# The V stage and the final norm of a hybrid block, token by token

## What is computed

```
q = (hf @ w_q).reshape(t, 8, 2, 128); s = einsum(q, sub_keys)
# per head: top 16 of each half, top 16 of their 256 sums -> 128 experts a token, of 16384
act = gelu(einsum('td,tkd->tk', x, u[idx]))
out = einsum('tk,tkd->td', gate * act, v[idx])
return rmsnorm(x + out, final_norm_w)
```

## Time and profile before

| | us |
|---|---|
| median of 3 runs | 5157.62 |
| the profiled execution | 5157.0 |
| its span, first to last instruction | 5155.2 |
| TensorE matmul busy in it | 4926.2 |
| VectorE busy | 3193.6 |
| ScalarE busy | 1684.1 |
| GpSimd busy | 1115.2 |

### The profile page before, as it was taken

The page is one execution under the profiler, slowest core; times in us unless marked ns, Lnnn a source line. Parts: engine busy times, 40 slices in busy tenths (PEclk is TensorE's granted clock), DMA queues, the critical chain, the costliest instruction groups (busy, mean ns, idle before and its releaser), DMA issues. The chain is left out here.

```text
span 5155.2 us, 69591 instructions
## 1 busy us (share of the span) xinstructions
PE 4926.2 (96%) x25836; PEld 4445.1 (86%) x25836; DVE 3193.6 (62%) x4382; ACT 1684.1 (33%) x1716; POOL 1115.2 (22%) x454
## 2 busy tenths in 40 slices
PE   6999988999999899998969999999999899999997
PEld 5878767888888787787759999999999799999997
DVE  3566666888888100101038866666776688888886
ACT  2222323333333222222223248885222222222222
POOL 2433320000000344343334430001221111111111
PEclk6999989999999999999989999999999999999998
DMA  1222212222222332334223357778997888888884
GB/s 71 90 90 77 90 57 82 78 87 77 77 87 71 124 109 104 144 122 157 98 99 110 116 206 284 276 274 315 337 341 293 298 299 296 298 299 300 302 301 151
DMA packets 230894, 913.34 MB, mean 177 GB/s; under 512 B 18352, under 2 KB 100912, under 8 KB 152624
## 3 DMA queue, kind: packets, MB, share of 16 engines
q1 hardware_dynamic: 193968, 644.12, 35.0%
q0 software_dynamic: 36864, 268.45, 14.6%
HBM read 837.00 MB, written 75.50 MB: 177 GB/s over the span
## 5 line engine op out<-in xcount | busy, mean ns | idle before, releaser
L158 POOL TENSOR_TENSOR ring_low<-ring_raw,ring_high 128x2048 fp32r<-128x2048 f32 x167 | 777.2, 4654 | 2178.9 <-ACT ring_high L153 2178.9
L176 PE MATMUL rt_acc<-h_high,ring_high 128*128 128x384 f32 (+1 forms) x2304 | 789.9, 343 | 0.7 <-POOL ring_low L158 0.7
L177 PE MATMUL rt_acc<-h_low,ring_high 128*128 128x384 f32 (+1 forms) x2304 | 784.4, 340 | 0.0
L178 PE MATMUL rt_acc<-h_high,ring_low 128*128 128x384 f32 (+1 forms) x2304 | 784.2, 340 | 0.0
L153 ACT ACTIVATE ring_high<-ring_raw 128x2048 fp32r<-128x2048 f32 x337 | 645.6, 1916 | 391.2 <-PE out_acc L178 125.1
L176 PEld LDWEIGHTS rt_acc<-h_high,ring_high 128*128 128x128 f32 x2304 | 433.1, 188 | 10.9 <-POOL ring_low L158 1.0
L177 PEld LDWEIGHTS rt_acc<-h_low,ring_high 128*128 128x128 f32 x2304 | 433.1, 188 | 9.9
L178 PEld LDWEIGHTS rt_acc<-h_high,ring_low 128*128 128x128 f32 x2304 | 432.8, 188 | 10.1
L176 PE MATMUL hg_acc<-h_high,ring_high 128*128 128x512 f32 x1024 | 408.1, 399 | 9.2 <-DVEq L968 9.2
L178 PE MATMUL hg_acc<-h_high,ring_low 128*128 128x512 f32 x1024 | 401.0, 392 | 0.0
L177 PE MATMUL hg_acc<-h_low,ring_high 128*128 128x512 f32 x1024 | 399.7, 390 | 0.0
(11 more groups left out here) (300 smaller groups left out, 10136.8 us busy)
## 6 DMA issues: line engine op xcount, KB each, us to landing
ring_raw<-u_tiles SPq DMA_DIRECT2D x128, 1024.0 KB, 5.1
ring_raw<-v_tiles SPq DMA_DIRECT2D x128, 1024.0 KB, 5.8
ring_raw<-w_hg SPq DMA_DIRECT2D x64, 1024.0 KB, 4.8
ring_raw<-w_ssd SPq DMA_DIRECT2D x48, 1024.0 KB, 4.8
ring_raw<-w_mix_s SPq DMA_DIRECT2D x32, 1024.0 KB, 4.8
ring_raw<-w_mix_h SPq DMA_DIRECT2D x32, 1024.0 KB, 4.8
gelu<-sb_rt_gelu SPq DMA_DIRECT2D x128, 192.0 KB, 5.1
gates<-sb_rt_table SPq DMA_DIRECT2D x12, 2048.0 KB, 7.7
```

The costliest lines, as they stand in the source:

```text
L158: nc.gpsimd.tensor_tensor(ring.low[:, slot], ring.raw[:, slot], ring.high[:, slot].bitcast(F32), ALU.subtract).then_inc(ring.low_ready, 1)
L176: nc.tensor.matmul(out, high[:, m], x_high[:, k, tokens], start=(k == 0), stop=False, skip_group_check=True)
L177: nc.tensor.matmul(out, high[:, m], x_low[:, k, tokens], start=False, stop=False, skip_group_check=True)
L178: last = nc.tensor.matmul(out, low[:, m], x_high[:, k, tokens], start=False, stop=(k == KT - 1), skip_group_check=True)
```

## The change

The V stage and the final norm work with tokens on partitions: `x_tok` is `[128, 4 token blocks, 2048]`. In the V stage w's 128x128 blocks (keys by tokens) are the stationary side and 512 columns of v the moving one, so a half has 6 outputs (3 token blocks by 2 pieces of 512 features) in place of 8, over eight banks in turn. The gathered rows are added right into `x_tok`'s block 0. The out stage turns each x_mid tile by four transposes and stores it to DRAM as `x_tok`, in place of the copy of x_mid in the ffn norm. The first group's inputs, `weigh`, w's high and low are done in the last turns of the U part; the `gate_table` buffer of the route stage becomes one of the outer scope. x_tok lands in two halves by features, gathers wait for the first, and group 0's lows of tiles 2 and 3 stand ahead of VectorE's wait for it. Groups 0 to 7 are written out, the others loop. The final norm is done on VectorE within the last half, with the root on ScalarE and a store per token block and half; the host side no longer transposes the output. Shortened:

```diff
+class Weights:       # gelu, w, gate, high0, low0 on the right side of SBUF
+    def load(self, sp, scratch, g, landed):   # two DMAs: gelu and gates of group g
+    def weigh(self, vec):                     # w = gelu * gate, as weigh() before
 def out_stage(...)
+            def turn(n, slot):                                      # TensorE
+                pe.wait_ge(added, n + 3)
+                pe.wait_ge(turn_read, n + 1)
+                for c in range(NC):
+                    last = nc.tensor.transpose(ps_turn[slot][:, c], x_mid[:, n, c * P:(c + 1) * P], const["ident"])
+                last.then_inc(turned, 1)
+            def keep(n, slot, before):                              # ScalarE
+                act.wait_ge(turned, n + 1)
+                act.wait_ge(tok_stored[slot], 16 * before)
+                nc.scalar.activation(tok[:, slot], ps_turn[slot][:], ACT.Copy).then_inc(turn_read, 1)
+            def store(n, slot):                                     # SP, after load_tile(n + 4)
+                sp.wait_ge(turn_read, n + 3)
+                sp.dma_start(x_tok[:, :, ds(P * n, P)], tok[:, slot]).then_inc(tok_stored[slot], 16)
-            with pe.Fori(1, KT // 2) as i:
+            for i in range(1, KT // 2):
                 for s in range(2):
                     project(2 * i + s, s)
                     sum_squares(2 * i + (s - 1), 1 - s)
+                    turn(2 * i + (s - 1), 1 - s)
             sum_squares(KT - 1, 1, stop=True)
+            turn(KT - 1, 1)
 def norm_stage(...)
-            if keep is not None:
-                sp.dma_start(keep, src[:]).then_inc(stored, 16)
 def route_stage(...)                                                # SP
+            sp.wait_ge(table_stored, 16 * (BLOCKS + 2))
+            for s in range(2):
+                sp.wait_ge(gelu_stored[s], 16 * (VGROUP // 2 + 1))
+            weights.load(sp, scratch, 0, v_landed)
             turn(PAIRS - 2, 1)
             load_ahead(sp, ring, FIRST + 2 * PAIRS, following)
@@ ScalarE
-            with act.Fori(FREE_PAIRS + GATE_PAIRS, PAIRS) as i:
+            with act.Fori(FREE_PAIRS + GATE_PAIRS, PAIRS - 1) as i:
                 pair(i)
+            act.wait_ge(v_weighted, 1)
+            nc.scalar.activation(weights.high0, weights.w, ACT.Copy).then_inc(v_split, 1)
+            pair(PAIRS - 1)
@@ VectorE
+                if j == 2 * LATE_PAIRS - 2:
+                    dve.wait_ge(v_landed, 32)
+                    weights.weigh(vec).then_inc(v_weighted, 1)
                 low(late + j, (j + 1) % 2)
+                if j == 2 * LATE_PAIRS - 2:
+                    dve.wait_ge(v_split, 1)
+                    vec.tensor_tensor(weights.low0, weights.w, weights.high0.bitcast(F32), ALU.subtract)
 def output_stage(...)                                               # SP
-            inputs(0)
+            weights.load(sp, scratch, 1, in_landed)
             for s in range(2, 4):
                 unit(0, s)
-            sp.dma_start(x_mid[:], scratch["x_mid"]).then_inc(x_landed, 16)
-            with sp.Fori(1, N) as g:
-                sp.wait_ge(weighted, g)
-                inputs(g)
-                for s in range(4):
+            for i in range(2):
+                sp.dma_start(x_tok[:, :, sl], scratch["x_tok"][:, :, sl]).then_inc(x_landed[i], 16)
+            with sp.Fori(1, N - 1) as g:
+                for s in range(2):
+                    unit(g, s)
+                sp.wait_ge(weighted, g)
+                weights.load(sp, scratch, g + 1, in_landed)
+                for s in range(2, 4):
                     unit(g, s)
@@ GpSimd
+            pool.wait_ge(x_landed[0], 16)
             for k in range(HK):
@@ ScalarE
+            nc.scalar.preload_act_table_set(EXP_LN_SET)
             high(0, 1)
@@ TensorE
-                    for d in range(OUTS):                            # OUTS was 8, is 6
-                        pe.wait_ge(out_added, 2 * OUTS * g + (OUTS * half + d + 1))
-                        o = ps_out[d][:, 0:REST]
+                    for i in range(OUTS):
+                        pe.wait_ge(out_added, 2 * OUTS * g + (OUTS * half + i + 1))
+                        o = ps_out[(2 * OUTS * buf + OUTS * half + i) % BANKS][:]
+                        toks = slice(i // 2 * CH, (i // 2 + 1) * CH)
                         for j in range(GROUP):
                             s = 2 * half + j // 2
+                            if i == 0 and j % 2 == 0:
+                                pe.wait_ge(ring.low_ready, ring.base + 4 * g + (s + 1))
+                            m = slice(j % 2 * HALF + i % 2 * T, j % 2 * HALF + (i % 2 + 1) * T)
+                            high, low = w_high[buf][:, j, toks], w_low[buf][:, j, toks]
+                            nc.tensor.matmul(o, high, v_high[s][:, m], start=(j == 0), stop=False)
+                            nc.tensor.matmul(o, low, v_high[s][:, m], start=False, stop=False)
+                            last = nc.tensor.matmul(o, high, v_low[s][:, m], start=False, stop=(j == GROUP - 1))
@@ VectorE, one half of a group
+                    for i in range(OUTS):
+                        s = 2 * half + i // 3
+                        if i in (0, 3) and not (first and half == 0):
+                            low(4 * g + (s + 2), (s + 2) % 4)
+                        if first and i == 0:
+                            if half == 0:
+                                low(2, 2)
+                                low(3, 3)
+                            dve.wait_ge(x_landed[half], 16)
+                        if i in (1, 4):    # a gathered row; group 0: rows 0 and 1, in its second half
+                            ...
+                        if i == 5 and half == 1 and static and 0 < g < STATIC - 1:
+                            row(5 * g + 1)                            # a fifth row in groups 1 to 6
+                        if i == 2 + half:  # half 0: weigh(g + 1); half 1: weights_low(g + 1)
+                            ...
+                        add_output(g, half, i, buf)                   # 128x512 into x_tok
@@ VectorE, the last half, after its first half's six adds
+            for c in range(NC):
+                square(c, 0)                                          # 128x1024, multiply and sum
+            square(0, 1)
+            ...                                                       # adds 0 and 1
+            square(1, 1); sum_of(1)
+            ...                                                       # adds 2 and 3
+            square(2, 1); sum_of(2); sum_of(0)
+            scale(1)                                                  # twice 128x1024: x * rstd * weight
+            add_output(last, 1, 4, 1)
+            scale(2)
+            add_output(last, 1, 5, 1)
+            square(3, 1); sum_of(3)
+            scale(0)
+            scale(3)
```

More of the change, by code:

```diff
@@ L180, in product, with norm_stage @@
     return last
-def norm_stage(nc, name, src, weight, work, ones, eps, load=None, split=None, store=None, ring=None,
-               first_tiles=None, keep=None, mean=None):
+def norm_stage(nc, name, src, weight, work, ones, eps, load=None, split=None, ring=None,
+               first_tiles=None, mean=None):
     with ExitStack() as ctx:
@@ L1329, in sum_squares @@
                 pe.wait_ge(squared, n + 1)
-                nc.tensor.matmul(mean[:], ones, square[:, slot], start=start, stop=stop,
+                nc.tensor.matmul(mean[:], const["ones"], square[:, slot], start=start, stop=stop,
                                  skip_group_check=True).then_inc(summed, 1)
@@ new lines, in row, with group @@
+            def row(k):
+                add_rows(k, k % 4, k // 4)
+            def group(g, buf, static):
+                for half in range(2):
+                    first = static and g == 0
+                    for i in range(OUTS):
[8 more added lines that the diff above has]
+                        if i in (1, 4):
+                            if not static or g == STATIC - 1:
+                                add_rows(4 * g + (4 + s), s, g + 1)
+                            elif g > 0:
+                                row(5 * g + (s - 3))
+                            elif half == 1:
+                                row(s - 2)
+                        if i == 5 and half == 1 and static and 0 < g < STATIC - 1:
+                            row(5 * g + 1)
+                        if i == 2 + half:
+                            if half == 0:
+                                dve.wait_ge(w_ready, g + 1)
+                                weigh(g + 1)
+                            else:
+                                weights_low(g + 1, 1 - buf)
+                        add_output(g, half, i, buf)
@@ new lines, in square, with sum_of, scale @@
+            def square(c, half):
+                sl = slice(half * HALF, (half + 1) * HALF)
+                chain.after(vec.tensor_tensor_reduce(spare[:], x_tok[:, c, sl], x_tok[:, c, sl], 1.0, 0.0,
```

(61 more changed lines are left out.)

220 lines of the change are left out of this document (125 added, 95 removed).

## The result

| | us |
|---|---|
| before, median of 4 runs beside it | 5157.90 |
| after, median of 4 runs (5108.31 to 5110.87) | 5109.23 |
| ratio, 95% interval | 0.9908 (0.9895 to 0.992) |
| forecast, with its range | 5097 (5087 to 5118) |
| the profiled execution after, its span | 5110.87, 5109.1 |

What follows compares the result with a forecast made beforehand. TensorE's step was taken to bound the V stage, VectorE next behind it. Terms -22.3 - 18.3 - 31.2 + 7.4 + 4.2 = -60.2 us took the 5157.6 us median to 5097 us, range 5087 to 5118.

Steps and rivals of the forecast that it cites:

- rival (a): V stage opening: gathers, tiles and x land late together; 5107 us, with late tiles in groups 1 to 6 up to 5118; chance 0.12.
- Stream: V stage: 4608 matmuls of 226.2 ns in place of 6144 of 173.3 ns, 1064.6 to 1042.3 us: -22.3 us.
- VectorE keeps up: V stage: VectorE needs 28.5 us of TensorE's 32.6 a group, 30.8 in groups 1 to 6; cost 0, up to +5 us.
- The DMA forecast: V stage: a load of 9.5 MB a group moves at 292 GB/s, 322 in groups 1 to 6.
- Opening: V stage's start: time over the stream falls from 30.0 to 11.7 us, -18.3 us.
- the two holes that were forecast: V stage's opening: TensorE idles once for 5 to 6 us and once for about 4.
- one hole back: V stage's opening: a hole like the old second one, 8.0 us with its restart 2.1, comes back: 5107 us.
- the ninth output: V stage's opening: due at 4048, needing only add 0 and the lows of tiles 2 and 3; no hole there, 8.0 us before.
- U stage: Group 0's inputs, weigh and w's high go ahead of the last U tile's work: 0, +1.5 or +4 us if cover fails.
- Out stage: Four transposes per tile, 0.49 us x 15: +7.4 us; last copy and store before the next stage: +4.2 us (3 to 8).
- Tail: After the last V matmul: the norm overlaps the last half, 14.5 us (12.5 to 19) in place of 45.7: -31.2 us.

Runs made afterwards that it cites:

- the lower buffers: The changed kernel with w's high and low of even groups from group 2 on moved to bytes 134432 to 159008 per partition: 5104.03 us.

## Why the prediction was right, and where not

Direction and size were right; the time lies in the range, 12 us above the forecast of 5097 and 3 us above what the forecast gave as its own range (5087 to 5106). It is inside the stated range by the room left for rival (a). Step by step:

- **Stream, -22.3 forecast, -15.1 measured** (4608 x 227.75 ns = 1049.5, against 1064.6). The mechanism was right: a matmul of 512 columns pays its fixed cost once for a third more columns. The step that was mis-sized is "I take the first, since it is a 512-column stream with a weight load per matmul too". Odd groups took 226.7 ns, which is the mix stage's own pace from start to start: the swapped roles cost nothing, and 2 us of the miss are in the 226.2, read from a count that takes in the matmuls at the ends of its 200 us. Even groups took 228.9, 5 us more, for the place of their stationary operand, as the lower buffers, which gave 5.3 back, show. The Trainium skill, TensorE: Matmul & The Clock Gate, "Back-to-back issue gap", gives the 215.8 ns at 512 columns for a matmul by itself, and about 131 ns for a sustained stream of weight loads and matmuls; the prediction used the first for a stream, and these 226.7 agree with neither.
- **VectorE keeps up: right.** It was 94% busy in groups 1 to 6 and 88% later; no hole is released by it there. The DMA forecast, 292 GB/s and 322, was 301 and 337. Its 9.5 MB a group were of 1024 x 1024 bytes, that is 9.96 MB; 9.96 in 32.7 us are 305 GB/s, and with a fifth row 337.
- **Opening, -18.3 forecast, -10.1 measured.** From the last U matmul's end to the last V matmul's end are 1069.4 us, 19.9 over the stream, not 11.7. Without the third hole and its restart (8.7) it would be 11.2, so the two holes that were forecast are right in sum. The step that failed is "The next thing late is row 0, at about 4050, then lows 4, 5 and w's low for group 1, done about 4057, due 4059". On the clock of the stage's later start (first V matmul at 4031.34, not 4020.4) that is 4068, due 4070; w's low was done at 4075.9. The sum took tiles 4 and 5 as landing like a steady tile, 5.8 us; it took 18, because the gathers, which the change starts at that moment, share the engines by packets and not by need. (The change also cuts the residual's own packets from 32 KB to 4: before, from 4038 to 4048, SyncE's queue passed 109 of them, 3.57 MB, beside 112 of the gathers', 0.84 MB.) That was rival (a), at 10 us for "one hole back", where the opening missed by 8.2. Its reason was right; that its 5107 lies so near to 5109 is in part luck, since it has none of the stream's 7 us.
- **The lows ahead of the wait, and the halves.** The prediction gave the ninth output to them. The hole there is gone, but neither edit alone is what closed it: the residual's first half lands 11.6 us after its issue and not 25.0, ten us ahead of the ninth output, and undoing either costs nothing (both at once was not tried). The reading was also off by two outputs: the ninth needs add 0, but the lows of tiles 2 and 3 are needed where the second half begins, at the seventh. It began at 4053.2, and they were done by 4047.5, so this cost nothing; with them behind the wait they were done at 4053.7, half a microsecond ahead.
- **U stage: 0 forecast, 0.7 measured.** The last U matmul ends 11.0 us later than before, of which 10.3 are the out stage's.
- **Out stage, +7.4 and +4.2 forecast.** The steady steps grew by 0.45 us, where 0.49 was forecast, and the last add is 6.2 us later; the end grew by 4.1. Together the norm starts 10.3 us later, 11.6 forecast.
- **Tail, -31.2 forecast, -31.9 measured: right.** VectorE ends 9.0 us behind the last matmul, as the prediction had it.

The measured terms are -15.1 - 10.1 - 31.9 + 6.2 + 4.1 + 0.7 = -46.1, by which the profiled executions differ. Two terms miss, the stream by 7.2 and the opening by 8.2, both to the same side, and the others give 1.3 back.

## What to carry to other kernels

When a step starts a transfer at a new moment, work out who else's loads are queued then, and share the DMA engines by packets: here an 8 KB gather packet for each 4 KB tile packet took two thirds, and what comes in small packets gets least. With the DMA engines full, another order of the loads (the residual's half late) and of VectorE's instructions (the lows ahead of the wait) gained nothing here; keep the transfer that nobody needs yet out of it, by making it wait for the last one that is needed. Before taking the pace of one stream for another, compare where their operands lie, and take the pace from start to start and not from a count.

## What the hardware showed that I had not expected

- A matmul of 512 columns takes 226.7 ns with its stationary operand at 134432 to 159008 bytes of a partition and 228.9 at 186336 to 210912.
- The engines took the packets of two queues nearly one for one whatever their size: 8 KB against 4 KB (268 and 283), 512 B (273 against 354, and 13 of 4 KB) and 32 KB (112, some of them a few bytes, against 109).
- The DMA engines moved 414 GB/s in the mean for 28 us on end (4038 to 4066), with one queue and then with two.
- While gathers of 8 rows rather than 128 ran, the transfers beside them were slower: 240 GB/s at full engines. Why stays open.
